# One level of Strassen's scheme for the output projection of a hybrid decoder layer, with the sample tile moved ahead of the last head's transposes

## What is computed

```python
def mixer_layer(x, ...):
    ...
    y_conv = gb * yc * jax.nn.silu(zc)
    ...
    y_m = (h.astype(x.dtype) * jax.nn.sigmoid(o)) * jax.nn.silu(zm)
    out = jnp.einsum('btw,wd->btd', jnp.concatenate([y_conv, y_m], axis=-1), w_out)
    return x + out, ...

y_prompt = rmsnorm(xp[:, N_META:], final_norm_gain)      # (1, 2048, 1024)
y_sample = rmsnorm(xs, final_norm_gain)                  # (8, 8, 1024)
```

## Time and profile before

| | us |
|---|---|
| runs shown (3) | 1163.98 median, 1163.52 to 1165.56 |
| the profiled execution, its own time | 1166.93 |
| its span, from first to last instruction | 1165.3 |
| PE busy | 1115.3 (96%) |
| DVE busy | 487.3 (42%) |
| ACT busy | 323.8 (28%) |
| POOL busy | 101.2 (9%) |
| chain that ended last: PE's share | 88% |

### The profile page before, as it was taken

How to read it: one execution, slowest core, us unless ns; L and a number is a source line. 1 busy time by engine, 2 the same in 40 slices (tenths; PEclk the granted TensorE clock), 3 DMA queues, 4 the chain that set the end, 5 groups by cost and what they waited for, 6 DMA issues and landing times.

```text
span 1165.3 us, 19377 instructions
## 1 busy us (share of the span) xinstructions
PE 1115.3 (96%) x7378; PEld 631.6 (54%) x7378; DVE 487.3 (42%) x1010; ACT 323.8 (28%) x661; POOL 101.2 (9%) x182
## 2 busy tenths in 40 slices
PE   3889999999999999999999999999999998999996
PEld 2545555555656565656665555566555654444442
DVE  5766666565434332353433233533332343222222
ACT  5563344543312121333121213321211232011110
POOL 5000101000001000000010000001000001111011
PEclk8899999999999999999999999999999998999998
DMA  5231020014100000330000005300000132454451
GB/s 177 81 102 47 12 91 19 19 44 129 39 10 14 28 10 10 111 100 13 1 23 28 10 12 139 104 25 11 30 10 10 37 102 82 138 180 121 150 161 72
DMA packets 81910, 72.86 MB, mean 63 GB/s; under 512 B 6881, under 2 KB 72565, under 8 KB 81813
## 3 DMA queue, kind: packets, MB, share of 16 engines
q1 hardware_dynamic: 43376, 36.04, 10.4%
q10 hardware_dynamic: 32340, 15.78, 4.9%
q0 software_dynamic: 6096, 19.79, 4.7%
HBM read 51.80 MB, written 19.78 MB: 61 GB/s over the span
## 4 chain that ended last, share of the span: by engine, by line
PE 88%; DVE 7%; ACT 2%; issue 1%; POOL 1%; DMA 0%; ACTq 0%; DVEq 0%; SPq 0%; POOLq 0%
PE bank L563 18%; PE bank L565 18%; PE bank L564 18%; PE bank L798 5%; PE bank L800 5%; PE bank L799 5%; PE bank L572 2%; PE bank L574 2%; PE bank L573 2%; PE bank L621 1%; PE bank L646 1%; PE bank L641 1%; PE bank L691 1%; PE bank L640 1%; PE bank L594 1%
## 5 line engine op out<-in xcount | busy, mean ns | idle before, releaser
L564 PE MATMUL bank<-xTl,Wh 128*128 128x512 f16 (+1 forms) x1280 | 420.7, 345 | 0.0
L563 PE MATMUL bank<-xTh,Wh 128*128 128x512 f16 (+1 forms) x1280 | 418.3, 346 | 2.4 <-DVE xtmp L155 2.4
L565 PE MATMUL bank<-xTh,Wl 128*128 128x512 f16 (+1 forms) x1280 | 420.5, 345 | 0.0
L565 PEld LDWEIGHTS bank<-xTh,Wl 128*128 128x128 f16 x1280 | 126.3, 99 | 122.2 <-issue 2.2
L563 PEld LDWEIGHTS bank<-xTh,Wh 128*128 128x128 f16 x1280 | 126.3, 99 | 111.0 <-issue 5.0
L564 PEld LDWEIGHTS bank<-xTl,Wh 128*128 128x128 f16 x1280 | 126.5, 99 | 109.0 <-issue 3.5
L572 PE MATMUL bank<-Wh,xTh 128*128 128x128 f16 x544 | 93.8, 220 | 3.5 <-DVE zs L155 3.0
L574 PE MATMUL bank<-Wh,xTl 128*128 128x128 f16 x544 | 93.9, 220 | 0.0
L573 PE MATMUL bank<-Wl,xTh 128*128 128x128 f16 x544 | 93.8, 220 | 0.0
L155 ACT ACTIVATE junk<-xs 128x1024 f16<-128x1024 f32 (+2 forms) x34 | 35.9, 1056 | 162.4 <-DVE xs L155 159.6
L155 DVE SCALAR_TENSOR_TENSOR xs<-bank,xs 128x512 f32<-128x512 f32 (+1 forms) x34 | 23.5, 691 | 99.8 <-PE bank L800 99.8
(11 more groups left out here) (249 smaller groups left out, 1299.0 us busy)
## 6 DMA issues: line engine op xcount, KB each, us to landing
xs<-in_x_prompt SPq DMA_DIRECT2D x32, 512.0 KB, 3.6
wst<-in_w_in ACTq DMA_DIRECT2D x27, 512.0 KB, 3.8
y_mid<-yst POOLq DMA_DIRECT2D x32, 256.0 KB, 2.5
out<-wst POOLq DMA_DIRECT2D x16, 512.0 KB, 4.3
wst<-in_w_in SPq DMA_DIRECT2D x9, 512.0 KB, 4.4
wst<-in_w_out SPq DMA_DIRECT2D x8, 512.0 KB, 3.6
xTl<-y_mid SPq DMA_DIRECT2D x32, 128.0 KB, 2.7
xTh<-y_mid SPq DMA_DIRECT2D x32, 128.0 KB, 3.4
```

What stands on the lines that cost most here:

```text
L563: mm(out, wh[:, k, :], xh, start=(k == 0), stop=False)
L564: mm(out, wh[:, k, :], xl, start=False, stop=False)
L565: last = mm(out, wl[:, k, :], xh, start=False, stop=(k == KT - 1))
```

## The change

The output projection of the prompt is cut in 8 units of 256 tokens (two row tiles). With A the gated results of a unit in quarters (rows: first or second 128 tokens; columns: the convolution group's 512 channels or the memory group's) and B the quarters of `w_out`, a unit is seven products of 128 x 512 by 512 x 512 in place of eight (Winograd's form). Each is 4 x 3 = 12 matmuls of 512 columns.

- **Operand sums of y.** In every block of every head DVE makes four sums of quarters S1 to S4 (`ysum`, four instructions of 128 x 256) in `heads_out`, ahead of the low part of `dp`; ACT casts them (`sums_high`, 128 x 1024, at the half of GC), DVE makes their low parts (`sums_low`, at the end of HC), and POOL stores them as a third store of the block. All go to a new DRAM scratch `y_ops`, laid out by unit, in rows that one load can take. `zs` and `G` share the buffer of `ysum`.
- **Operand sums of w.** The last block takes `w_out` in 8 slabs (256 columns of each of four quarters). Of a slab POOL makes four differences T1 to T4 in a chain (`output_sums`: 128 x 256 each, into one buffer `wtmp`), ACT casts two pieces of the raw slab and, after POOL, two of the sums (256, 512, 768, 256 elements), and DVE makes the four low parts. POOL begins a slab only when DVE has ended the one before, since `wtmp` is single.
- **Order.** The sample tile stands ahead of the last transposes, with 40 matmuls (its high and low rows are one operand of 128 rows, so that two matmuls replace three). Each unit's first product is made during the unit before.
- **Projection's end.** POOL adds the first product to three quarters of the residual (`residuals`), DVE adds a bank as each product ends, some banks are read while further products are summed into them. SP loads y for a unit in 4 DMAs, and two residual tiles; there are two sets of buffers for each.

The core of the diff, mean and power of the norm left out:

```diff
+SLABS = {V: (0, 1), Q: (2,), GC: (3,), HC: (4,), GB: (5,), ZC: (6,), O: (7,)}
...
+            def output_sums(slab):
+
+                pool.wait_ge(w_in_s[slab % STAGES], slab_loads(slab))
+                pool.wait_ge(wo_low, slab)
+                raw = w_raw(slab)
+                b11, b12, b21, b22 = raw[:, 0, 0, :], raw[:, 0, 1, :], raw[:, 1, 0, :], raw[:, 1, 1, :]
+                for op, x, y in ((B_T1, b12, b11), (B_T2, b22, wtmp[:, B_T1, :]), (B_T3, b22, b12), (B_T4, b21, wtmp[:, B_T2, :])):
+                    pool.tensor_tensor(wtmp[:, op, :], x, y, ALU.subtract).then_inc(wo_sums, 1)
+                    pool.wait_ge(wo_sums, 4 * slab + op + 1)
...
+            def residuals(n):
+
+                pool.wait_ge(r_in[n % 2], 32 * (n // 2 + 1))
+                pool.wait_ge(p1_copied, n + 1)
+                z1, z2 = Z[n % 2]
+                for part in (z1[:, BT:D], z2[:, BT:D], z2[:, 0:BT]):
+                    pool.tensor_tensor(part, part, p1s[n % 2], ALU.add).then_inc(x_plus, 1)
...
+            first_product(0)
+            for n in range(UNITS):
+                one, two, three = CHAINS[n % 2]
...
+                product(n, two, S2, B_T2, True)
+                if n > 1:
+                    pe.wait_ge(c12_out, n - 1)
+                product(n, three, S1, B_T1, True)
+                pe.wait_ge(p1_copied, n + 1)
+                product(n, one, A12, B_21, False)
+                pe.wait_ge(s6_out, n + 1)
+                product(n, two, S3, B_T3, False)
+                if n < UNITS - 1:
+                    first_product(n + 1)
+                pe.wait_ge(u7_out, n + 1)
+                product(n, two, A22, B_T4, False)
+                pe.wait_ge(c22_out, n + 1)
+                product(n, three, S4, B_22, False)
...
+            def output_high(slab):
+
+                i, q = slab // 2, slab % 2
+                raw, sums = w_raw(slab), (w_sums(xTh, i, 0, q), w_sums(xTh, i, 1, q))
+                act.wait_ge(w_in_s[slab % STAGES], slab_loads(slab))
+                did(fn(w11[0][:, i * BT + q * 2 * P:i * BT + (q + 1) * 2 * P], raw[:, 0, 0, :], ACT.Copy, scale=WS))
+                did(fn(sums[1][:, 1:3, :], raw[:, 1, :, :], ACT.Copy, scale=WS))
+                act.wait_ge(wo_sums, 4 * slab + 4)
+                did(fn(sums[0], wtmp[:, 0:3, :], ACT.Copy, scale=WS))
+                mark(fn(sums[1][:, 0, :], wtmp[:, 3, :], ACT.Copy, scale=WS).then_inc(wo_high, 1), wo_high, slab + 1)
...
+            act.wait_ge(smp_added, 4)
+            b_square(0, zsmp[0:DB * DS, :], DB * DS)
+            p1_copy(0)
```

More of the change, by code:

```diff
@@ L499, in pool_block @@
                         x_power(1 + CH * (b + 1) + c)
+                if following == "output weights":
+                    for slab in range(5):
+                        output_sums(slab)
+                if not (first and b == 0):
+                    store_sums(g if b else g - 1, b - 1 if b else NB - 1)
                 if b == 0:
@@ L507, in pool_block @@
                     pool.dma_start(dst, cs[:, :, 0:P]).then_inc(cs_out, 16)
+                if following == "output weights":
+                    for slab in range(5, 7):
+                        output_sums(slab)
                 store_y(g, b, 0)
+                if following == "output weights":
+                    output_sums(7)
                 pool.wait_ge(h_ms, nth(g, b) + 1)
@@ L785, in _ @@
             pe_block(H - 1, NB - 1, False)
+            pe.wait_ge(wo_low, 8)
+            pe.wait_ge(smp_y_in, 16 * KT)
+            use_t1(T1_END)
+            pe.wait_ge(p_free[0], H * NT * NB // 2)
+            for h in range(2):
+                terms = [(i, i, B_11) for i in range(H)]
+                terms += [(i, i, B_T1) for i in range(H)] if h else []
+                terms += [(H + i, i, B_22 if h else B_21) for i in range(H)]
+                for k, i, op in terms:
+                    mm(SMP[h][:, :], ysmp[:, k, :], w_operand(xTh, i, op), start=(k == 0 and op == B_11), stop=False)
+                    last = mm(SMP[h][:, :], ysmp[:, k, :], w_operand(xTl, i, op), start=False, stop=(k == KT - 1))
+                last.then_inc(smp_full, 1)
@@ L924, in at_half @@
                     heads_high(g, b, t0(g, b, "hT", first))
+                if t == GC and not (first and b == 0):
+                    sums_high(g, b)
                 if t == GC and b == 0:
@@ L1379, in at_end @@
                     mark(tt(dp[:, :], dp[:, :], S[:, :], ALU.mult).then_inc(s_free, 1), s_free, n * 3 + 1)
+                if t == HC and not (first and b == 0):
+                    sums_low(g, b)
                 if t == ZC:
@@ L1571, in _ @@
[L1571 to L1577 removed]
+                mark(stt(z, z, rsx[0:n, tile:tile + 1], fgain[0:n, :], ALU.mult, ALU.mult).then_inc(b_out, 1), b_out, tile + 1)
```

388 lines of the change are left out of this document (269 added, 119 removed).

## The result

The changed kernel takes **1180.17 us** (median of 4 runs, 1177.45 to 1181.50), the kernel before 1164.77 beside it (4 runs): ratio 1.013, 95% interval 1.0107 to 1.0153. It is slower by 1.3%, and 1.2 us above the predicted range. Its profiled execution took 1181.09 with a span of 1179.5; before these were 1166.93 and 1165.3.

What follows compares the result with a forecast made beforehand. PE was taken as the bound, except in the first blocks, the heads-to-projection join and the end. Saved products (-20.7 us) and the other terms, chiefly +18.3 for slabs, summed to +2.3: median 1166.4 us, range 1152 to 1179.

Steps and rivals of the forecast that it cites:

- Operand sums in the heads: DVE's y sums: free in heads 1 to 3, +0.5 us (0 to 3) in the first head.
- growth before 915: Sign against the forecast: the heads before 915 us have grown.
- Slab chain: Last block: serial POOL, ACT and DVE work, 7.0 us a slab, delays the sample tile's start by 18.3 us.
- Sample tile: Between heads and projection: 40 matmuls plus slow clock take 11.3 us in place of 13.2, -1.9.
- transposes: The last transposes, until now inside PE's wait, stand behind the sample tile: +0.6 us.
- P2's wait: Behind the sample tile PE waits for ACT's first-product copy: +2.5 us, and +2.1 for the lowered clock.
- last unit: Projection's last unit has no next product between two that use one bank: +1.2 us.
- End: After the last matmul: 4.5 us in place of 4.8, -0.3.
- B: Slab chain: differences at 0.475 us, start 3.5 us earlier, clock kept after short stalls; 1157.5 us, chance 0.22.
- C: Differences at 0.855 us, start 4.4 later, residual-buffer loop makes PE wait in the last five units; 1177.5 us, chance 0.22.
- A: Last block: a slab takes at most a PE tile, 5.2 us, so PE covers the weights; 1146 us, chance 0.10.
- D: Projection: y loads at 231 GB/s arrive 1 to 2 us late in six units; 1174 us, chance 0.06.

Runs made afterwards that it cites:

- the fastest kernel: On the kernel combining all edits with a reordered tail, POOL takes slabs 0 and 1 before the second y store, 2 to 7 before the sums' store; 1151.44 us.
- The narrow run: POOL's four differences per weight slab made only 8 columns wide, against the changed kernel, so the prompt output is wrong; 1169.11 us.

## Why the prediction was wrong

Against the profiled execution before, the sum said +2.3 and +14.2 was measured. Of the 11.9 us between them the first head has 6.9, the slab chain 3.2 and the program's end 1.6. Term by term:

- **Operand sums in the heads, +0.5 (0 to 3): the step that failed.** The price per block was right (four at 0.42 to 0.43 and 1.23), and so was "PE covers this: 0" for heads 2 to 4. For the first head I looked for PE's next need of DVE's *sums* and named the K transpose and HC's bank. What PE waits for there is the other work on DVE, `xtmp` and `cs`, which the sums push back in program order: PE's waits for these two grew by 4.6 us. The clock fell behind one of the three stalls only. DVE was also not a third busy there, as in the later heads (222.80 of 615.00 us), but 188.4 of the first 305 us, 62%. Measured +7.6 (7.4 by means), of which taking the DVE work away returns 5.5 (313.50, 310.39, 307.99), and of the medians 5.6 (1180.17, 1178.20, 1174.53); the upper bound of 3 was far too low, and some 3 us of the growth have no cause shown. The prediction named growth before 915 as what would make it wrong, and that happened.
- **Slab chain, +18.3.** Right mechanism, size off by 3.2: the start is 28.95 later, 7.4 of it from the heads, so +21.5. The period was 7.27 for 7.0, 1.9 over the seven steps: a difference takes 0.72 to 0.73, not 0.665. Three steps were held up by 2.3 us in all, where 1.1 was said, and the last slab came 0.7 sooner than its terms. The other 0.9 is POOL's start: 940.20 - 7.4 = 932.8 for 931.9. That is a slip of addition: the prediction's own terms, 930.13 + 0.69 + 1.9, give 932.7. PE's waits came as said, 3.6 us for `u` and 9.2 for the first update, and besides 3.5 for Q's result (`qf`), which was not listed.
- **Sample tile -1.9, transposes +0.6, P2's wait +2.5 with +2.1 of clock, last unit +1.2.** The tile took 11.28 (11.3 said), the wait 3.1, the clock behind it 0.74 from 1028 to 1032, and the last unit's wait 0.8. From the sample's start to the last matmul -16.2 was forecast with the products, -16.1 measured (179.2 to 163.1); so close a sum is in part luck, since the wait was 0.6 longer and the last unit's 0.4 shorter.
- **End, -0.3.** From the last matmul to the last issue it is 4.85 us where it was 4.96 (1171.97 - 1167.12, 1159.16 - 1154.20), near enough. But the last two stores are now issued 1.66 us apart, 1170.31 and 1171.97, and from the last issue to the span's end it takes 7.5 us where it was 6.2, in the fastest kernel too. That the first store holds up the second is not shown. The end is +1.3 in all.

Two workings of the prediction are off without moving its sum. At the rate that it takes from the Trainium skill (GPSIMD Engine Reference, Performance versus the Vector engine), 4497 ns for 2048 elements, 256 elements are an estimated 0.56 us; its 0.65 needs a fixed part as well, and 0.72 was measured. And the shifts of 3.5 and 4.4 us in B and C are not derived: differences 0.19 us cheaper or dearer change eight slabs by 6.1. The narrow run moved the sample tile by 10.9 of the 16.6 us that its POOL rows saved (8 x 4 x 0.52), so two thirds is what came through.

Of the rivals, A and B needed cheap differences, and there are none. C gave 1177.5, near the time, by another mechanism: its residual loop did not occur, an addition is 1.24, and PE waits 0.8 us in the last unit, 0.2 in an early one. D did not occur either. The forecast had no rival for the first head, the one term that failed by more than its bound.

The premise that the placement of the slabs decides was right: narrow differences alone take 11.1 us off the whole, and an order made for it, with the first head and the tail mended too, wins 1.2% over the kernel before. The 20.7 us of products were always there.

## What to carry to other kernels

When work is added to an engine that has room on average, read its busy share stretch by stretch (here 36% in the later heads, 62% in the first) and ask in each what stands *behind* it in program order and who waits for that, not only who needs the added result: the same 2.9 us a block cost nothing in heads 2 to 4 and 5.5 us in the first head. Hand a chain of engines two buffers and a head start where the first one idles before giving up on it; the largest gains here (8, 6 and 7 us) were order and one spare buffer. An edit that removes one wait can uncover the next instruction in the same queue, as the copy's and the slab table's did, so look at what is late next before counting it.

## What the runs showed of the hardware

**POOL and DVE hold each other up.** The `yc` group, DVE's rows in the change, and then with POOL's differences narrow:

```profile
970.59 0.84 DVE L161 TENSOR_SCALAR yc<-u,par 128x512 f32<-128x512 f32 x1
971.54 2.15 DVE L161 SCALAR_TENSOR_TENSOR yc<-u,par,yc 128x512 f32<-128x512 f32 x2
```

```profile
962.25 0.49 DVE L161 TENSOR_SCALAR yc<-u,par 128x512 f32<-128x512 f32 x1
962.85 1.54 DVE L161 SCALAR_TENSOR_TENSOR yc<-u,par,yc 128x512 f32<-128x512 f32 x2
```

POOL's 0.72 became 1.05 in the same place (972.09), and up to 1.33 in the kernel with two buffers. DVE's low parts of 512 elements there took 1.10 in place of 0.69. DVE's rows that read one tensor from PSUM (`u<-bank,gcs`, `kw<-bank,sel`) stayed at 0.69 beside POOL (969.79 and 954.68 in the change). By the Trainium skill (SBUF - State Buffer, "SBUF: two separate sides") a GpSimd operation that reads SBUF excludes a DVE operation with two SBUF inputs, and any GpSimd operation one in a two-port mode, and the other way round; the runs agree, and the prediction's "No run here shows it" is answered: in the fastest complete kernel it costs at most 4 us, by the run with narrow differences, whose gain also holds POOL's own shorter time.

**POOL's price.** A difference of 8 columns is 0.20 us, of 256 is 0.72, an addition of 512 is 1.24: about 2.1 ns an element and 0.18 us fixed. The forecast's middle of one and two inputs' price (1.48 and 2.97 ns) was 8% low.
